# Differential attention in fp32: where z is transposed and how the head norm reaches it

## The reference

```python
h = rms_norm(x, norm_g)
q, k, v, z = jnp.split(h @ w_in, 4, axis=-1)          # 1024 -> 4 x 2048
q = rms_norm(q.reshape(b, s, 16, 2, 64), q_norm_g) * (64 ** -0.5)
k = rms_norm(k.reshape(b, s, 16, 2, 64), k_norm_g)
v = v.reshape(b, s, 16, 128)
...
scores = jnp.einsum('bqhmd,bkhmd->bhmqk', qb, kb)
probs = jax.nn.softmax(scores + bias[None, :, None], axis=-1)
weights = probs[:, :, 0] - lam * probs[:, :, 1]
o = jnp.einsum('bhqk,bkhe->bqhe', weights, vb)
...
o = rms_norm(o, head_norm_g) * (1.0 - lam_0)          # over the 128 values of a head
o = o.reshape(b, s, 2048) * jax.nn.silu(z)
return x + o @ w_out                                   # 2048 -> 1024
```

## Time and profile before

| what | value |
|---|---|
| timed runs | 1274.62, 1275.55, 1276.28 us, median 1275.55 us |
| span of the profiled execution | 1280.3 us |
| PE busy | 1273.9 us, 99% of the span |
| DVE, ACT, POOL busy | 792.3, 612.0, 298.6 us |
| span that belongs to the second attention with its output projection | from about 731 us to the end |
| TensorE clock granted | full in every stretch |

### The profile page before, as it was taken

The page is one execution under the profiler, slowest core; times in us unless marked ns, Lnnn a source line. Parts: engine busy times, 40 slices in busy tenths (PEclk is TensorE's granted clock), DMA queues, the critical chain, the costliest instruction groups (busy, mean ns, idle before and its releaser), DMA issues.

```text
span 1280.3 us, 18355 instructions
## 1 busy us (share of the span) xinstructions
PE 1273.9 (99%) x7170; PEld 1086.2 (85%) x7170; DVE 792.3 (62%) x1578; ACT 612.0 (48%) x1300; POOL 298.6 (23%) x203
## 2 busy tenths in 40 slices
PE   9999999999999999999999999999999999999999
PEld 6788888888899999999888888888888888888787
DVE  5435665443479977877333647676767667677743
ACT  4436654333445444445233445556565555656531
POOL 2023310000055656540001412131312223131110
DMA  6322232233533334243236322222223222223511
GB/s 235 108 58 75 59 99 70 96 98 99 203 127 102 107 122 122 77 133 114 72 110 214 116 66 72 93 74 74 75 74 101 89 75 75 74 76 127 184 59 66
DMA packets 110441, 130.35 MB, mean 102 GB/s; under 512 B 7569, under 2 KB 87697, under 8 KB 110354
## 3 DMA queue, kind: packets, MB, share of 16 engines
q1 hardware_dynamic: 104594, 112.39, 27.3%
q10 hardware_dynamic: 5760, 16.78, 3.6%
HBM read 119.72 MB, written 9.44 MB: 101 GB/s over the span
## 4 chain that ended last, share of the span: by engine, by line
PE 96%; DVE 2%; DMA 0%; issue 0%; ACT 0%; POOL 0%; SPq 0%; DVEq 0%
PE ps L928 17%; PE ps L930 16%; PE ps L929 16%; PE ps L933 7%; PE ps L934 6%; PE ps L935 6%; PE ps L1165 5%; PE ps L1163 5%; PE ps L1166 5%; PE ps L1221 3%; PE ps L1231 1%; PE ps L1203 1%; PE ps L1255 1%; DVE wlo L1610 1%; PE ps L1246 1%; PE ps L1245 1%
## 5 line engine op out<-in xcount | busy, mean ns | idle before, releaser
L1610 DVE TENSOR_TENSOR wlo<-raw,whi 128x512 fp32r<-128x512 f32 (+1 forms) x294 | 232.0, 815 | 188.1 <-ACT whi L1292 187.4
L1292 ACT ACTIVATE whi<-raw 128x512 fp32r<-128x512 f32 (+2 forms) x338 | 208.4, 649 | 116.7 <-PE ps L930 88.3
L928 PE MATMUL ps<-whi,hth 128*128 128x512 f32 x592 | 242.2, 409 | 0.2 <-DVE wlo L1610 0.2
L930 PE MATMUL ps<-wlo,hth 128*128 128x512 f32 x592 | 231.4, 391 | 0.0
L929 PE MATMUL ps<-whi,htl 128*128 128x512 f32 x592 | 231.2, 391 | 0.0
L2044 POOL TENSOR_TENSOR wlo<-raw,whi 128x384 fp32r<-128x384 f32 (+1 forms) x44 | 49.1, 1134 | 415.7 <-ACT whi L1292 415.7
L928 PEld LDWEIGHTS ps<-whi,hth 128*128 128x128 f32 x592 | 111.3, 188 | 26.5 <-issue 5.2
L930 PEld LDWEIGHTS ps<-wlo,hth 128*128 128x128 f32 x592 | 111.2, 188 | 24.5
L929 PEld LDWEIGHTS ps<-whi,htl 128*128 128x128 f32 x592 | 111.6, 189 | 19.1
L933 PE MATMUL ps<-hth,whi 128*128 128x512 f32 (+1 forms) x288 | 111.5, 387 | 0.0
L934 PE MATMUL ps<-htl,whi 128*128 128x512 f32 (+1 forms) x288 | 108.9, 378 | 0.0
(11 more groups left out here) (362 smaller groups left out, 2913.6 us busy)
## 6 DMA issues: line engine op xcount, KB each, us to landing
raw<-in_l_w_in SPq DMA_DIRECT2D x64, 512.0 KB, 4.5
raw<-in_w_gate_up SPq DMA_DIRECT2D x44, 512.0 KB, 4.7
raw<-in_w_in SPq DMA_DIRECT2D x13, 1024.0 KB, 5.1
raw<-in_w_down SPq DMA_DIRECT2D x10, 1024.0 KB, 4.9
raw<-in_l_w_out SPq DMA_DIRECT2D x8, 1024.0 KB, 5.0
raw<-in_w_in SPq DMA_DIRECT2D x26, 256.0 KB, 3.4
raw<-in_w_branch SPq DMA_DIRECT2D x8, 512.0 KB, 3.9
raw<-in_w_out SPq DMA_DIRECT2D x4, 1024.0 KB, 4.9
```

What stands on the lines that cost most here:

```text
L928: e.matmul(o, ah, wh[:, cs], start=a, stop=False)
L930: m = e.matmul(o, ah, wl[:, cs], start=False, stop=z)
L1292: return e.activation(out, in_, ACT.Copy, **how)
L1610: return e.tensor_tensor(out, src, hi_part.bitcast(F32), ALU.subtract)
```

## The change

The second weight part of a group no longer holds v and z of this group. In an even group it holds v of this group and the next (512 columns of v, tokens standing, step `vs`); in an odd group it holds z of four heads, with the weights standing and the tokens moving, so that z comes out transposed, one head per bank (step `zg`). v has three buffers for two before, z five single tiles `zg` for two double ones.

The copy `oc` and the transposes of `og` are gone. DVE multiplies the head's result by gain and z straight from the bank into `oz` (step `p2`, after ACT's squares). The norm factor is one number per token and lies with tokens on partitions in `hn`; a transfer on ACT's queue writes its 512 numbers of 4 bytes each as one row of a scratch tensor in DRAM (step `rs`), a second one waits for the first and reads that row back to all 128 partitions, 256 KB, into `rbc` (step `rl`), and DVE multiplies `oz` by it (step `to`). `to` stands one or two steps later than before. The last part of the output projection begins with the first halves of its four units (they use heads 12 and 13) before their second halves (heads 14 and 15). When the program is made, one buffer size is given (`dynamic_dma_scratch_size=1024`), which leaves more room for these tiles.

```diff
-            for a in (0, 2):
-                for k in (0, 4):
-                    self.add(4, 512, [(256 * i, 4, 0, kview(w_in2, k, 4, E2 * (a + i) + 256 * g, 256))
-                                      for i in range(2)])
+            for k in (0, 4):
+                self.add(4, 512, [(256 * i, 4, 0, kview(w_in2, k, 4, E2 * i + 256 * g, 256)) for i in range(2)])
+            for k in (0, 4):
+                self.add(4, 512, [(0, 4, 0, kview(w_in2, k, 4, E2 * (2 + g % 2) + 512 * (g // 2), 512))])
...
-        for c in range(2):
-            finish(self.w2_units(c, 3))
+        firsts = [self.unit(W.w2[0, 3], 16, 4, "w2", 0, 3, tb) for tb in range(TB)]
+        for u in firsts:
+            next(u)
+        for tb, u in enumerate(firsts):
+            finish(u)
+            put("yo", 0, 3, tb)
+        finish(self.w2_units(1, 3))
...
                 if i == 1:
-                    self.put("vz", g, tb)
+                    self.put(("vs", "zg")[g % 2], g, tb)
...
         self.scores(even, 2)
         self.scores(odd, 0)
-        yield
+        if past:
+            put("rs", even - 2)
+        yield
+        if past:
+            put("rl", even - 2)
         put("cb", even, 2)
         yield
+        put("cb", even, 3)
+        yield
         if past:
-            put("to", even - 2, bank())
-        put("cb", even, 3)
-        yield
+            put("to", even - 2)
         put("cb", odd, 0)
         put("ab", odd + 1)
         yield
...
         self.scores(odd, 1)
         self.scores(odd, 2)
-        yield
         if past:
-            put("t2", even, 2, bank())
-            put("to", even - 1, bank())
-        else:
-            put("t2", even, 2, bank())
+            put("rs", even - 1)
+        yield
+        if past:
+            put("rl", even - 1)
+        put("t2", even, 2, bank())
         put("cb", odd, 2)
         yield
         put("p2", even, bank())
         put("cb", odd, 3)
         yield
+        if past:
+            put("to", even - 1)
         yield
...
+        self.put("rs", 15)
+        yield
+        self.put("rl", 15)
+        yield
+        self.put("to", 15)
...
+                    n = W.at + 4 * g + 2 * vz + i
+                    if vz and g % 2:
+                        three(n, ps[PJ[tb]][:, :], P * tb, False, HTH, HTL, 4 * i, EVERY, i == 0, i == 1, R4,
+                              i0).then_inc(mm, 1)
+                        free[PJ[tb]] = [(z_d, 2 * (g - 1) + tb + 1)]
+                    else:
+                        three(n, ps[PJ[tb]][:, :], 0, True, HTH, HTL, 4 * i, slice(P * tb, P * tb + P), i == 0, i == 1,
+                              R4, i0).then_inc(mm, 1)
+                        free[PJ[tb]] = ([(v2_lo, 4 * g + 2 * tb + 2)] if vz else
+                                        [(qsq_a, 4 * g + tb + 1), (qn_d, 4 * g + tb + 1)])
...
-                    pe.wait_ge(vz_d, 8 * g + 8)
+                    pe.wait_ge(v2_lo, 8 * (g // 2) + 8)
...
-                    free[b] = [(oc_a, 2 * h + 2)]
+                    free[b] = [(oz_d, h + 1)]
...
-                elif kind == "to":
-                    h, b = a
-                    claim(b)
-                    pe.wait_ge(og_p, h + 1)
-                    for qb in range(TB):
-                        m = e.transpose(ps[b][:, P * qb:P * qb + P], og[:, qb, :], ident[:])
-                    m.then_inc(to_pe, 1)
-                    free[b] = [(ot_d2, h + 1)]
...
+                    for i in range(2):
+                        if g + i >= 3:
+                            act.wait_ge(p2_pe, 2 * (g + i - 3) + 2)
+                        copy(v2h[(g + i) % 3][:, tb, :], ps[PJ[tb]][:, 256 * i:256 * i + 256]).then_inc(v2_hi, 1)
+                elif kind == "zg":
+                    g, tb = a
+                    h = 2 * (g - 1) + tb
+                    act.wait_ge(mm, MM["pj", g, 1, 1, tb, 2])
+                    act.wait_ge(ht_lo, HT_ALL(2))
+                    for q in range(TB):
+                        act.wait_ge(x_out[q], 32)
+                    if h >= 5:
+                        act.wait_ge(oz_d, h - 4)
+                    e.activation(zg[h % 5][:], ps[PJ[tb]][:, :], ACT.Tanh, scale=0.5).then_inc(z_a, 1)
...
-                    act.wait_ge(to_pe, h)
-                    act.wait_ge(ot_d2, h)
-                    copy(oc[:], ps[b][:, :]).then_inc(oc_a, 1)
-                    e.activation(osq[:], ps[b][:, :], ACT.Square).then_inc(oc_a, 1)
+                    act.wait_ge(ss_pe, h)
+                    e.activation(osq[:], ps[b][:, :], ACT.Square).then_inc(osq_a, 1)
+                elif kind == "rs":
+                    h, = a
+                    act.wait_ge(hpow_p, h + 1)
+                    e.dma_start(r_row(h).rearrange("(q p) -> p q", p=P), hn[:, 8 * (h % 2) + 4:8 * (h % 2) + 8],
+                                allow_slow_non_contiguous=True).then_inc(r_out[h % 2], 16)
+                elif kind == "rl":
+                    h, = a
+                    act.wait_ge(r_out[h % 2], 16 * (h // 2 + 1))
+                    if h >= 2:
+                        act.wait_ge(ot_d2, h - 1)
+                    e.dma_start(rbc[h % 2][:], row_bc(r_row(h), S)).then_inc(r_in[h % 2], 16)
...
+                    for i in range(2):
+                        dve.wait_ge(v2_hi, 4 * g + 2 * tb + 2)
+                        lower(v2l[(g + i) % 3][:, tb, :], ps[PJ[tb]][:, 256 * i:256 * i + 256],
+                              v2h[(g + i) % 3][:, tb, :]).then_inc(v2_lo, 1)
+                elif kind == "zg":
+                    g, tb = a
+                    h = 2 * (g - 1) + tb
+                    z = zg[h % 5][:]
+                    dve.wait_ge(z_a, h + 1)
+                    e.scalar_tensor_tensor(z, z, 1.0, ps[PJ[tb]][:, :], ALU.add, ALU.mult).then_inc(z_d, 1)
...
+                elif kind == "p2":
+                    h, b = a
+                    dve.wait_ge(osq_a, h + 1)
+                    dve.wait_ge(z_d, h + 1)
+                    if h >= 2:
+                        dve.wait_ge(ot_d2, h - 1)
+                    e.scalar_tensor_tensor(oz[h % 2][:], ps[b][:, :], gh[:, 1:2], zg[h % 5][:], ALU.mult,
+                                           ALU.mult).then_inc(oz_d, 1)
                 elif kind == "to":
-                    h, b = a
-                    dve.wait_ge(to_pe, h + 1)
-                    dve.wait_ge(oc_a, 2 * h + 1)
+                    h, = a
+                    dve.wait_ge(oz_d, h + 1)
+                    dve.wait_ge(r_in[h % 2], 16 * (h // 2 + 1))
                     if 2 <= h < 14:
                         dve.wait_ge(ot_out[h % 2], 16 * (h // 2))
                     elif h >= 14:
                         dve.wait_ge(ot_hi, h - 13)
-                    e.scalar_tensor_tensor(ots[h % 2][:], oc[:], gh[:, 1:2], ps[b][:, :], ALU.mult,
-                                           ALU.mult).then_inc(ot_d2, 1)
+                    e.tensor_tensor(ots[h % 2][:], oz[h % 2][:], rbc[h % 2][:], ALU.mult).then_inc(ot_d2, 1)
...
-                    rb = hn[:, 4:8].rearrange("p (a d) -> p a d", d=1).to_broadcast([P, TB, P])
+                    o = 8 * (h % 2)
                     pool.wait_ge(hvar_d, h + 1)
-                    pool.wait_ge(to_pe, h)
-                    e.tensor_tensor(hn[:, 4:8], hn[:, 0:4], neghalf[:, 0:4], ALU.pow).then_inc(hpow_p, 1)
-                    pool.wait_ge(hpow_p, h + 1)
-                    pool.wait_ge(vz_d, 8 * (h // 2) + 8)
-                    e.tensor_tensor(og[:], zs[(h // 2) % 2][:, :, P * (h % 2):P * (h % 2) + P], rb,
-                                    ALU.mult).then_inc(og_p, 1)
+                    if h >= 2:
+                        pool.wait_ge(r_out[h % 2], 16 * (h // 2))
+                    e.tensor_tensor(hn[:, o + 4:o + 8], hn[:, o:o + 4], neghalf[:, 0:4], ALU.pow).then_inc(hpow_p, 1)
```

79 lines of the change are left out of this document (36 added, 43 removed).

## The result

The changed kernel takes 1395.44 us (median of 4 runs, 1393.89 to 1398.42) against 1275.65 for the kernel before (1274.62 to 1276.28): 1.0934 times as long, 95% interval 1.0909 to 1.0959. The forecast was 1270.9, faster, with a range up to 1282.0.

What follows compares the result with a forecast made beforehand. PE was taken to bound the kernel: 7.0 us of transposes saved, less 1.7 at `qn_f` and 0.6 at `p2`, gives 4.7 us off 1275.55, or 1270.9 us; range 1268.2 to 1282.

Steps and rivals of the forecast that it cites:

- Rival 1: Write lands late at ACT's waits ahead of `pth` and the scaling; slower from L = 3.84, 1282.2 at 4.4; chance 0.24.
- L: Time from the start of the factor write (`rs`) to its landing; taken as 3.3 us, ends 2.3 and 6.0.
- The formula: Gain in us against L: 7.0 - 1.7 - 6(L - 3.6) - 6(L - 3.2), each bracket only where positive.
- twelve places: Six even-head places (`qn_f`, free up to L = 3.6) and six odd-head places (`p2`, free up to 3.2).
- the last four heads with the end: Heads 12 to 15: no wait, all four keep their 0.44 us; margin 5 us at the kernel's end.
- break-even of 3.84 us: The L at which the forecast gain is zero; beyond it the kernel is slower.
- the transposes' worth: Removing the `og` transposes (L1262) takes 0.44 us per head off PE, 16 heads, 7.0 us.
- the charge at `qn_f`: At six even-head places PE comes early and waits for DVE's `qn_f`: 0.29 x 6 = 1.7 us of saving lost.
- The write's early issue: ACT's queue runs ahead of the engine, so the write starts after DVE's last maximum, not after the exponentials.
- PE's places: PE gaps ahead of the transposes of `qn_f` (under 0.4 us) and in `p2` of even heads (at most 0.1).
- the read back: Read of 256 KB into `rbc` (`rl`): DVE's wait, two or more steps behind, was taken as met.
- rivals 2 to 4: Write just covered, 1273 to 1278 (0.14 with the last); whole 7.0 saved, 1268.5 (0.12); z-tile matmuls slower, 3.8 us.

Runs made afterwards that it cites:

- e16: e1 with 12 ScalarE copies into a spare tile per head where it waited for the write; 1394.44 us.
- e15: Changed kernel with the factor write in 256 pieces of 8 B side by side, wait kept, read taking an input's row; 1282.37 us.
- e1: Changed kernel without the factor write and the waits for it, the read taking a row of an input instead; 1269.81 us.
- e2: Changed kernel with the write kept but ScalarE's wait for it left out, the read taking an input's row; 1279.51 us.
- e7: Changed kernel with the 4 B write kept, `rl` some three steps and `to` some five steps behind `rs`; 1286.37 us.

## Why the prediction was wrong

**The step that failed** is "The nearest by shape and number of pieces is 3.3 us, and that is what I take; 2.3 and 6.0 are the ends." The landing was 9.0 us, outside both ends. The row taken as nearest was a load; the same shape as a store into neighbouring 4 B of DRAM took nearly three times as long, and the prediction had warned of it ("a write of single numbers may cost more than a load of them") without letting it move the upper end. Rival 1 had the mechanism, the places and the sign, at 0.24, with a price at L = 4.4 and not at 9.

**The formula had the right slope and was not whole.** At L = 9.0 it gives 5.3 - 6 x 5.4 - 6 x 5.8 = -61.9 us, 1337. At its twelve places it is nearly right: 67.2 us by it, 73.0 us by the rows (37.0 at `qn_f`, and 46.7 less 10.7 for the last heads at `p2`). Missing were the last four heads with the end, 16.9 us, which it called looser and free, and the clock, most of the 36.6 us of longer busy time, which it didn't have at all: it counted a gap at its length. e16 gives nearly the same sum with no transfer. e15 tests it near its break-even: at 3.4 us it says 1271.5, measured 1282.4. Its span is 12.2 us over e1's: 7.6 us are waits, of them one gap of 3.8 us in the last heads (and three of 1.2 us at `p2`), 3.6 us are longer busy time, and 1.1 us is idle time in the first 100 us, which the change does not touch. So the break-even of 3.84 us was too kind as well.

**Right:** the transposes' worth. 5.6 us came with e1 (4.7 forecast, 7.0 without the charge at `qn_f`; that gap of 0.29 us did not show in e1, and where the rest of the 7.0 stays is open: the 128 matmuls of L953 in the z tiles last 414 ns in the mean for 407 at L948, and 128 x 0.007 = 0.9 us is the most that this could be). The write's early issue, PE's places, the read back as harmless to PE once the write has landed (VectorE waits 4.6 us for it in all), the z tiles and the other edits at nothing (rivals 2 to 4 did not come).

**Not foreseen:** the 4 B pieces slow the weight loads beside them (e2, e7) and the read behind them (e2).
